# Twelve modulation panels moved from every second attention unit to every differential attention unit

## What is computed

```python
def adaln(cvec, w, b):
    return jnp.split(jax.nn.silu(cvec) @ w + b, 6, axis=-1)

# differential attention, 4 heads: two softmaxes per head, combined
s = jnp.einsum('bqhmd,bkhmd->bhmqk', qb, k).astype(F32) * (A_HD ** -0.5)
p = jax.nn.softmax(s, axis=-1)
p = p[:, :, 0] - lam * p[:, :, 1]
return jnp.einsum('bhqk,bkhe->bqhe', p.astype(v.dtype), v)
# dense / neighbourhood attention, 8 heads: one softmax per head
```

## Time and profile before

| what | value |
|---|---|
| median of 3 runs | 1604.62 us (1604.56 to 1607.74) |
| profiled execution | 1609.15 us, its span 1607.5 us |
| TensorE busy | 1473.5 us, 92% of the span |
| VectorE, ScalarE busy | 1050.4 us, 898.1 us |
| granted TensorE clock over the span | 0.961 of full speed |

### The profile page before, as it was taken

How to read it: one execution, slowest core, us unless ns; L and a number is a source line. 1 busy time by engine, 2 the same in 40 slices (tenths; PEclk the granted TensorE clock), 3 DMA queues, 4 the chain that set the end, 5 groups by cost and what they waited for, 6 DMA issues and landing times.

```text
span 1607.5 us, 19117 instructions
## 1 busy us (share of the span) xinstructions
PE 1473.5 (92%) x7385; PEld 1219.7 (76%) x7385; DVE 1050.4 (65%) x1273; ACT 898.1 (56%) x1062; POOL 93.7 (6%) x162
## 2 busy tenths in 40 slices
PE   5989798899999998998797899999999999999991
PEld 1978346699998877886476788888888888888881
DVE  1533545542334445786666779798897989879794
ACT  2431446542223336593355668676686776867773
POOL 0312410000000001000002000000000000000001
PEclk7999899999999998999998999999999999999996
DMA  9692982134333224234806899999999999999993
GB/s 360 199 406 98 353 297 71 55 103 140 122 115 148 105 79 138 98 105 160 304 21 237 327 365 399 377 389 382 379 399 375 399 381 382 391 369 400 381 375 130
DMA packets 146621, 414.52 MB, mean 258 GB/s; under 512 B 6924, under 2 KB 30888, under 8 KB 146408
## 3 DMA queue, kind: packets, MB, share of 16 engines
q1 hardware_dynamic: 134192, 375.93, 63.0%
q0 software_dynamic: 9600, 34.07, 5.8%
q10 hardware_dynamic: 2744, 3.36, 0.6%
HBM read 391.29 MB, written 22.95 MB: 258 GB/s over the span
## 4 chain that ended last, share of the span: by engine, by line
PE 82%; DVE 9%; ACT 3%; DMA 3%; issue 1%; POOL 1%; ACTq 0%; POOLq 0%; DVEq 0%
PE bank L1893 40%; PE bank L1630 11%; PE bank L1422 6%; PE bank L1641 6%; PE bank L1474 4%; PE bank L1363 3%; PE bank L1419 3%; PE bank L1563 2%; DMA ring<-in_w_in_even_dram 1%; PE bank L1598 1%; PE bank L1861 1%; PE bank L1585 1%; DVE arena L2274 1%; DVE ring_parts L1982 1%; PE bank L1387 1%
## 5 line engine op out<-in xcount | busy, mean ns | idle before, releaser
L1893 PE MATMUL bank<-arena_parts 128*128 128x512 f32 x1520 | 400.1, 391 | 0.9 <-DVE arena_parts L2592 0.9
L1893 PEld LDWEIGHTS bank<-arena_parts 128*128 128x128 f32 x1520 | 283.8, 188 | 62.3 <-issue 2.5
L2585 DVE TENSOR_TENSOR ring_parts<-ring,arena_parts 128x2048 fp32r<-128x2048 f32 x124 | 278.4, 2287 | 70.8 <-ACT arena_parts L1265 70.8
L1265 ACT ACTIVATE arena_parts<-ring 128x2048 fp32r<-128x2048 f32 x124 | 234.0, 1919 | 29.5 <-DMA ring<-in_moe_w_dram 29.2
L1893 PE MATMUL bank<-ring_parts,arena_parts 128*128 128x512 f32 x720 | 222.9, 391 | 0.0
L1893 PEld LDWEIGHTS bank<-ring_parts,arena_parts 128*128 128x128 f32 x720 | 135.7, 188 | 28.7
L1630 PE MATMUL bank<-ht_parts,arena_parts 128*128 128x384 f32 x352 | 118.3, 336 | 0.4 <-DVE xn_parts L1993 0.3
L1630 PE MATMUL bank<-ht_parts,ring_parts 128*128 128x384 f32 x352 | 117.6, 334 | 0.0
L1630 PE MATMUL bank<-xn_parts,arena_parts 128*128 128x384 f32 x352 | 117.6, 334 | 0.0
L1893 PE MATMUL bank<-xn_parts,arena_parts 128*128 128x512 f32 x320 | 93.5, 394 | 6.3 <-DVE ring_parts L2585 6.3
L2209 DVE TENSOR_TENSOR arena<-arena,bank 128x384 f32<-128x384 f32 x22 | 12.2, 554 | 125.4 <-PE bank L1630 125.4
(11 more groups left out here) (429 smaller groups left out, 2678.6 us busy)
## 6 DMA issues: line engine op xcount, KB each, us to landing
ring<-in_moe_w_dram SPq DMA_DIRECT2D x184, 1024.0 KB, 7.0
arena<-in_moe_w_dram SPq DMA_DIRECT2D x60, 1024.0 KB, 6.7
ring<-in_mod_w_dram SPq DMA_DIRECT2D x24, 2048.0 KB, 8.9
ring<-in_ff_w_dram SPq DMA_DIRECT2D x23, 1024.0 KB, 7.9
ring<-in_w_in_even_dram SPq DMA_DIRECT2D x6, 2048.0 KB, 12.1
ring<-in_w_in_odd_dram SPq DMA_DIRECT2D x6, 2048.0 KB, 8.2
ring<-in_ff_w_dram SPq DMA_DIRECT2D x5, 2048.0 KB, 7.8
routed<-arena POOLq DMA_DIRECT2D x1, 7168.0 KB, 29.0
```

The source lines that it names most:

```text
L1265: act.activation(whi_moe[n_ % E_WHI], e_half(j, h), ACT.Copy).then_inc(whi_ready, 1)
L1893: ins = pe.matmul(bank[base + b][:, :], lhs[:, c_, :], rhs[:, k, 512 * b:512 * b + 512], start=(first and h == 0 and k == 0 and n_ == 0), ...
L2585: dve.tensor_tensor(e_half(j, h, low=True), e_half(j, h), whi_moe[(2 * j + h) % E_WHI], ALU.subtract).then_inc(wlo_ready, 1)
```

## The change

The panels 4 to 15 are now multiplied one in each of the bodies 0 to 11, that is in every body of a differential unit, and turned in bodies 1 to 12. TensorE makes the product at the end of its body and the turn at the place where it was. ScalarE's copy of the bank moves to the head of the next body, ahead of the exponentials. VectorE's code is as it was; only `turn_at` gives other numbers. The list of panels and SyncE's program are the same.

```diff
         def mod_at(i):
-            return 4 + i // 2 if i % 2 == 0 and i < 24 else None
+            return 4 + i if i < 12 else None

         def turn_at(i):
-            return 4 + i // 2 if i % 2 == 1 and i < 24 else None
+            return 3 + i if 1 <= i < 13 else None
...
             for i in range(NU + 1):
+                if turn_at(i) is not None:
+                    if i == 1:
+                        act.wait_ge(roped, 8)
+                    keep_mod(turn_at(i))
                 if i < NU:
...
-                if mod_at(i) is not None:
-                    if i == 0:
-                        act.wait_ge(roped, 8)
-                    keep_mod(mod_at(i))
                 if i >= 1:
...
                 if i + 1 < NU:
                     scores(i + 1)
-                m = mod_at(i)
-                if m is not None:
-                    mod_mm(m)
                 if turn_at(i) is not None:
                     mod_turn(turn_at(i))
...
                     ins.then_inc(pv_done, 1)
+                if mod_at(i) is not None:
+                    mod_mm(mod_at(i))
```

## The result

The changed kernel takes 1654.07 us (median of 4 runs, 1650.46 to 1657.74) against 1605.03 for the kernel before: a ratio of 1.0302, 95% interval 1.0274 to 1.0330. The forecast was 1622.6, with a range up to 1631. The direction was right, the size was not: 49 us came where 18 were expected.

The account below looks back on a forecast made before the run. TensorE was taken to bound the one-softmax units, a closed engine ring the differential ones. Panel 15's product ends at 238.3, then 22.7 us: body 24 at 261.0 instead of 243.0, 18.0 later, so 1604.62 becomes 1622.6 us; range 1611 to 1631.

Parts of the forecast that it names:

- The bound of each stage: TensorE bounds the units of one softmax; in the differential units it waits for VectorE's softmax arithmetic, queued behind `add_mod`.
- The ring: Differential bodies: product, copy, turn, `add_mod`, softmax arithmetic, transposes, value product in a closed loop; the product's 1.86 us is uncovered.
- The differential stage: Bodies 1 to 11: each becomes an odd body of before plus a product; panel 15's product ends at 238.3.
- The wait for panel 7: Differential bodies: panel 7 is wanted at 178.6 but lands at 180.3, so TensorE waits 1.8 us, once.
- paid spells: Lower-clock periods after waits in bodies 2 to 11: six, the first free, five at 1.3 us, 6.5 us.
- The panels: Panel 7 lands 18.8 us after it is sent for; later ones every 5.4 us, so transfers get ahead.
- the load of three queues: SyncE's panels, ScalarE's outputs and GpSimd's bias tiles together delay panel 7; with SyncE's queue alone, 1.8 us less.
- Body 12: Turn and `add_mod` of panel 15 still stand ahead of unit 11's arithmetic: 4.78 us, as body 3.
- The clock in the units of one softmax: Bodies 13 to 23 take 1.63 us each, 17.9 us; from body 24 the lists are the same, nothing given back.
- the forecast's own signs of being wrong: Panel waits in most bodies, bodies under 5.5 us, clock 0.50 over whole bodies, or one-softmax bodies still 2.4 us without modulation.
- The rival "TensorE at the lower clock through the whole stage": Differential stage: ten spells at 1.6 us and the clock down into body 12, 29 us later, 1633.6 us; chance 0.11.

Follow-up runs that it names:

- a burst: Changed kernel with 24 extra dense 128x384 products on TensorE at the end of body 13, read by nobody: 1633.12 us, ratio 1.0166 to the kernel before.
- a late product: Changed kernel with panel 15 multiplied in body 16 and turned in body 17 instead of 11 and 12: 1629.21 us, ratio 1.0152 to the kernel before.
- a made wait: Kernel before with seven extra ScalarE copies ahead of the exponentials of unit 25, so TensorE stands still in body 26: 1621.62 us, ratio 1.0095.
- the two bursts: Changed kernel with extra products at the end of body 13: 24 dense of 128x384, 1633.12 us; or 12 of the scores' kind (64 rows, fp32), 1671.57 us.

## Why the prediction was wrong

Its steps one by one, in the profiled executions.

- The bound of each stage: right. The ring held in the differential bodies (the waits above, twelve of them), and opening it removed them.
- The differential stage: the mechanism right. The product of panel 15 was to end at 238.3 and ended at 238.4; the stage had begun 1.5 us earlier (work ahead of it, at 150 us, lay as much earlier already), so it was 1.7 us longer than forecast. That the two ends agree to 0.1 us is luck. From the end of panel 5's product on, the bodies took 238.4 - 164.9 = 73.5 us where 238.3 - 167.8 = 70.5 had been put, but panel 5's product ended 2.9 us earlier than put: 1.5 by the earlier begin, the rest because it ran at the upper clock. The wait for panel 7 was 3.07 us (forecast 1.8). Five products ran at the lower clock and took 7.3 us more together; the forecast had put 6.5 for all its paid spells, and had the one behind panel 7's wait as free, where that product took 3.64 us instead of 1.92. Body 7 took 5.83 us where 4.23 + 1.86 = 6.09 had been put. Two bodies lay outside the 5.7 to 8 us that were to show the forecast right: body 3 with the wait for panel 7 (11.3 us) and body 4 (8.5 us).
- The panels: right. Panel 7 landed 18.7 us after its issue (18.8 in the earlier trace rows), not in some 8, and one is waited for. That the load of three queues was the reason was not tested.
- Body 12: 244.35 - 238.44 = 5.9 us, forecast 4.8; about 1.0 of the difference is its transposes and value products, which already ran at the lower clock.
- **The clock in the units of one softmax: wrong, and this is the step that failed.** The forecast said of bodies 13 to 23 that they "take 11 x 1.63 = 17.9" and of all behind them that "the lists are the same". They took 275.31 - 244.35 = 31.0 us, and bodies 24 to the gate rows 314.41 - 275.31 = 39.1 us instead of 267.61 - 243.00 = 24.6 in the kernel before. That is 13.1 and 14.5 us. Two of the forecast's own signs of being wrong came with it: a clock of 0.50 over whole bodies, and bodies of one softmax that take 31.0 / 11 = 2.8 us without modulation work.

The terms add up: 18.0 forecast, 1.7 in the differential stage, 1.1 in body 12, 13.1 and 14.5 make 48.4; less the 1.5 us by which the stage began earlier, 46.9, against 46.7 between the spans.

The rate of 1.63 us came from bodies that ran at a clock of 1.00, and I took it for a property of the bodies. It was a property of bodies that had entered at the upper clock. I had written that a spell at the lower clock follows a wait of 2 us in four cases of six, and had priced it at 1.3 us, because every spell in that trace was short. Each of those four spells holds a modulation product, and the runs show that it is this that kept them short. The change takes the products out of twelve bodies and leaves a wait of 2 us as the last thing before them; the spell then has no end. Removing that wait gives back 29 us, a burst 21, a late product 25, and a made wait in the kernel before costs 16.

The rival "TensorE at the lower clock through the whole stage" was the nearest, and it too ended the low clock at body 12: its 29 us were in the wrong stage. What I should have asked of the earlier trace rows is what stands behind the last wait, and whether it can raise the clock.

The Trainium skill (TensorE: Matmul & The Clock Gate, "What's actually happening") says that the clock is throttled by default and that activity releases the throttle. The runs bear out the release for the dense burst and for a modulation product. They do not bear it out for any activity: in the changed kernel TensorE was busy for 61.0 of the 61.0 us from 244 to 305, and the clock stayed at the lower level.

## What to carry to other kernels

A wait costs more than its length where the work behind it cannot raise TensorE's clock: look behind the last wait of a stage for such work, and price the stage at either level. Spread the work that raises the clock (here the modulation products) through the stages that cannot do it themselves, rather than finish it early. And before work is added to a body, see what it is queued ahead of on the engine that closes the loop: moving two small instructions behind the softmax arithmetic was worth 46 us in the changed kernel and 4 in the one before.

## What the runs showed of the hardware

- The granted clock had a memory: the bodies of one softmax kept TensorE busy all the time in both cases (61.0 of 61.0 us in the changed kernel, 31.95 of 32.0 in the one with the burst) and ran at 0.50 where they were entered at 0.50, from 242.2 to 317.3, and at 1.00 where they were entered at 1.00, from 248.0 to 288.9.
- 24 matmuls of 128x384 on all 128 rows raised it, 1.4 us after the first of them, and so did one modulation product (eight matmuls of 512 columns), 4.5 us after its start. Some 16 us of fp32 products with 64 rows did not. Which property counts was not separated: the two bursts differ in rows and in data type (the operands of the first are fp32r), and the modulation product, fp32 like the scores, in rows and columns.
- A standstill of 3.06 us brought it down before it was over (at 248.9), and waits of about 2 us brought it down in many cases, not in all. In the changed kernel it fell in or within 1.1 us behind five of the twelve waits for the arithmetic (1.80 to 2.13 us), and not behind the longest, 2.23 us. So the length of a wait does not settle it, and the rest stays open; in the wait of body 12, 2.13 us, the clock fell in all three traces that have it with no modulation product behind (the changed kernel and the two with bursts).
